# Half-width column groups beside SSD and mLSTM, ScalarE leads for a layer's first operands, and buffer clearing moved behind later weight splits

## The reference, cut to what matters

```python
hn = rms_norm(h, attn_norm_g[l])
proj = hn @ w_in[l]                      # 5056 columns, split among four mixers
y_a = mla_mixer(...)                     # latent attention, 8 heads
y_b = ssd_mixer(...)                     # Mamba-2 SSD, both directions, chunks of 128
y_c = diff_mixer(...)                    # differential attention
y_d = mlstm_mixer(...)                   # mLSTM, both directions, chunks of 128
h = h + concatenate([y_a, y_b, y_c, y_d], -1) @ w_out[l]
hn = rms_norm(h, ffn_norm_g[l])
gate, up = split(hn @ w_ffn_in[l], 2)
h = h + (silu(gate) * up) @ w_ffn_out[l]
```

## Time and profile before

| | us |
|---|---|
| median of three runs | 2256.19 |
| lowest, highest | 2255.35, 2264.37 |
| profiled execution | 2260.73 |
| its span in the trace | 2258.9 |

### The profile page before, as it was taken

One profiled execution on the slowest core, in us unless ns is written; L12 is line 12 of the kernel. 1 busy time (PEld: TensorE's weight loads), 2 busy tenths in 40 slices (PEclk: granted clock), 3 DMA queues, 4 the chain that ended last, 5 costly groups with the idle time before them and its releaser, 6 DMA issues.

```text
span 2258.9 us, 32608 instructions
## 1 busy us (share of the span) xinstructions
PE 2062.5 (91%) x13298; PEld 1781.2 (79%) x13298; DVE 1063.1 (47%) x1653; ACT 820.8 (36%) x1344; POOL 993.5 (44%) x593
## 2 busy tenths in 40 slices
PE   7989998888778999999999999997877789999999
PEld 7978887567657999999989878884555567888887
DVE  8532355565664744442038332555655656444400
ACT  3322343576554222222224322443664633222221
POOL 4455432784311444444434454335861334444444
PEclk9999999999998999999999999999998999999999
DMA  4211111000001222233222111111000012333333
GB/s 161 66 56 57 57 46 67 10 1 19 29 12 37 85 94 87 91 94 94 94 85 84 57 57 57 48 38 56 1 7 31 19 56 94 94 94 98 97 103 112
DMA packets 40035, 143.79 MB, mean 64 GB/s; under 512 B 4432, under 2 KB 4560, under 8 KB 39760
## 3 DMA queue, kind: packets, MB, share of 16 engines
q1 hardware_dynamic: 39888, 141.72, 19.6%
HBM read 139.60 MB, written 2.10 MB: 63 GB/s over the span
## 4 chain that ended last, share of the span: by engine, by line
PE 72%; DVE 11%; ACT 8%; issue 6%; POOL 2%; DMA 1%; SPq 0%; ACTq 0%; DVEq 0%; POOLq 0%
PE pb L850 44%; PE pb L885 6%; PE pb L886 6%; PE pb L887 6%; ACT ebuf L1468 2%; PE pb L1287 1%; DVE rowmax L1926 1%; POOL parts L632 1%; PE pb L1295 1%; ACT rstd L1436 1%; PE pb L1227 1%; DVE proj L1858 1%; PE pb L987 1%; ACT ebuf L1479 1%; ACT parts L1524 1%
## 5 line engine op out<-in xcount | busy, mean ns | idle before, releaser
L632 POOL TENSOR_TENSOR parts<-raw,parts 128x1024 fp32r<-128x1024 f32 x248 | 602.5, 2430 | 829.0 <-ACT parts L1524 828.8
L850 PE MATMUL pb<-mix,parts 128*128 128x264 f32 x4608 | 670.7, 294 | 41.1 <-POOL parts L632 15.7
L850 PEld LDWEIGHTS pb<-mix,parts 128*128 128x128 f32 x4608 | 609.2, 193 | 68.0 <-issue 26.1
L1524 ACT ACTIVATE parts<-raw 128x1024 fp32r<-128x1024 f32 x248 | 262.5, 1058 | 851.1 <-PE pb L850 549.6
L850 PE MATMUL pb<-proj_r,parts 128*128 128x264 f32 x3104 | 429.2, 286 | 0.5 <-POOL parts L632 0.5
L850 PEld LDWEIGHTS pb<-proj_r,parts 128*128 128x128 f32 x3104 | 401.2, 189 | 0.8 <-issue 0.7
L885 PE MATMUL pb<-proj_r,parts 128*128 128x512 f32 x528 | 207.5, 393 | 0.8 <-DVE mbuf L1858 0.8
L887 PE MATMUL pb<-proj_r,parts 128*128 128x512 f32 x528 | 207.7, 393 | 0.0
L886 PE MATMUL pb<-proj_r,parts 128*128 128x512 f32 x496 | 198.1, 399 | 0.0
L1864 DVE TENSOR_TENSOR h<-h,pb 128x528 f32<-128x528 f32 (+1 forms) x48 | 33.2, 693 | 274.9 <-PE pb L850 143.9
L1858 DVE TENSOR_TENSOR mbuf<-pb,rstd 128x528 f32<-128x528 f32 (+1 forms) x44 | 30.8, 700 | 214.8 <-PE pb L850 110.5
(11 more groups left out here) (277 smaller groups left out, 2831.6 us busy)
## 6 DMA issues: line engine op xcount, KB each, us to landing
raw<-w_stream SPq DMA_DIRECT2D x250, 512.0 KB, 3.5
w_head<-w_heads SPq DMA_DIRECT2D x8, 512.0 KB, 4.9
h<-x_t SPq DMA_DIRECT2D x8, 264.0 KB, 6.8
out_t<-h SPq DMA_DIRECT2D x8, 256.0 KB, 4.7
con<-consts SPq DMA_DIRECT2D x1, 1652.5 KB, 10.5
par<-params SPq DMA_DIRECT2D x1, 340.0 KB, 4.3
con<-consts SPq DMA_DIRECT2D x1, 128.0 KB, 7.1
```

Source lines behind the costliest of these rows:

```text
L632: nc.gpsimd.tensor_tensor(parts[:, n % PARTS, 1, :], w, parts[:, n % PARTS, 0, :].bitcast(FP32), ALU.subtract).then_inc(split.sem, 1)
L850: last = nc.tensor.matmul(pb[rows_, 2 * p + a, 0:HALF], lhs_t, rhs[:, a * HALF:(a + 1) * HALF], start=start, stop=stop)
L1524: nc.scalar.activation(parts[:, n % PARTS, 0, :], raw[:, r % RAW, :], ACT.Copy).then_inc(lead_ready.sem, 1)
```

## The change

1. The 25 groups beside SSD and mLSTM are computed half by half. Pieces 0 and 1 of a group now do all eight input tiles for tokens 0 to 263 (one bank), pieces 2 and 3 for tokens 264 to 527 (the other bank). VectorE takes out each half by itself: half 0 at slot 4j+2, half 1 at slot 4j+4. Piece 0 waits for half 0 of the group before, piece 2 for half 1 of it.
2. ScalarE makes the leads of h times gain for both layers (`gain_lead`); VectorE makes only the rests (`gain_rest`). At the end of layer 0 the first four rests stand ahead of the last residual addition.
3. At the start SyncE issues the first weights, then eight columns of the parameters, then all eight tiles of h in a row, then the second weights and the rest. ScalarE loads its table and makes the first weight lead before it waits for parameters.
4. GpSimd clears the six buffers after the rests of slots 2, 4, 5 and 6 of layer 0.

```diff
@@ sync
+            sp.dma_start(raw[:, 0, :], w_stream[0, :, :]).then_inc(loaded[0].sem, 16)
+            sp.dma_start(par[:, 0, 0:KD], params[:, 0, 0:KD]).then_inc(gain_in.sem, 16)
             for k in range(KD):
-                if k < RAW:
-                    sp.dma_start(raw[:, k, :], w_stream[k, :, :]).then_inc(loaded[k].sem, 16)
                 sp.dma_start(h[:, k, :], x_t[:, k, :]).then_inc(x_in[k].sem, 16)
-                if k == 0:
-                    sp.dma_start(par[:, :, :], params).then_inc(par_in.sem, 16)
+            sp.dma_start(raw[:, 1, :], w_stream[1, :, :]).then_inc(loaded[1].sem, 16)
+            sp.dma_start(par[:, 0, KD:N_PARAM], params[:, 0, KD:N_PARAM]).then_inc(par_in.sem, 16)
+            sp.dma_start(par[:, 1:DEPTH, :], params[:, 1:DEPTH, :]).then_inc(par_in.sem, 16)
@@ gpsimd
-            nc.gpsimd.memset(v_tok[:, :], 0.0).then_inc(cleared.sem, 1)
...
-            nc.gpsimd.memset(rows2, 0.0).then_inc(cleared.sem, 1)
+            def clear(s):
+                for buf in ((), (), (mbuf[:, :, :], cols[:, :, :]), (), (v_tok[:, :],), (qh[:, :, :],), (o_tok[:, :, :], rows2))[s]:
+                    nc.gpsimd.memset(buf, 0.0).then_inc(cleared.sem, 1)
...
                     rest(l, s)
+                    if l == 0 and s < 7:
+                        clear(s)
@@ tensor
+            def half_piece(l, g, a, k0):
+                n = l * N_SLOT + g
+                if k0 == 0 and a == 0:
+                    pe.wait_ge(split.sem, n + 1)
+                    if g == G_SSD:
+                        pe.wait_ge(evac.sem, evac.at(l, g))
+                    else:
+                        pe.wait_ge(half_evac.sem, half_evac.at(l, g - G_SSD))
+                elif k0 == 0:
+                    pe.wait_ge(evac.sem, evac.at(l, g))
+                o, cut = pb[:, 2 * bank_pair(g) + a, 0:HALF], slice(a * HALF, (a + 1) * HALF)
+                for k in range(k0, k0 + KD // 2):
+                    w_lead, w_rest = (parts[:, n % PARTS, b, k * P:(k + 1) * P] for b in range(2))
+                    lead, rest = (ap[:, cut] for ap in xg_parts(k))
+                    nc.tensor.matmul(o, w_lead, lead, start=(k == 0), stop=False)
+                    nc.tensor.matmul(o, w_lead, rest, start=False, stop=False)
+                    last = nc.tensor.matmul(o, w_rest, lead, start=False, stop=(k == KD - 1))
+                if k0:
+                    done = w_used if a else half_done
+                    last.then_inc(done.sem, 1)
...
-                    k = (KD // PIECES) * (p % PIECES)
-                    beside(l, G_SSD + p // PIECES, 0, xg_parts, ((k, k + KD // PIECES),))
+                    half_piece(l, G_SSD + p // PIECES, p % PIECES // 2, KD // 2 * (p % 2))
@@ scalar
+            def gain_lead(l, k):
+                if l == 0:
+                    act.wait_ge(x_in[k].sem, 16)
+                else:
+                    act.wait_ge(evac.sem, evac.at(l - 1, G_FOUT + k + 1))
+                nc.scalar.activation(xg_parts(k)[0], h[:, k, :], ACT.Copy, scale=par_at(l, "attn_g", k)).then_inc(xg_lead.sem, 1)
...
-            act.wait_ge(par_in.sem, 16)
+            nc.scalar.preload_act_table_set("natural_log_exp_and_others")
+            lead(0, 0)
+            act.wait_ge(gain_in.sem, 16)
             act.wait_ge(eps_ready.sem, 1)
             for l in range(DEPTH):
                 if l == 0:
-                    nc.scalar.preload_act_table_set("natural_log_exp_and_others")
                     for k in range(KD):
-                        act.wait_ge(x_in[k].sem, 16)
+                        gain_lead(l, k)
+                        if k == 4:
+                            lead(l, 1)
+                    for k in range(KD):
                         residual_square(l, 0, k)
-                        if k < PARTS:
-                            lead(l, k)
-                lead(l, 2)
+                        if k == 3:
+                            lead(l, 2)
+                else:
+                    lead(l, 2)
...
                 for s in range(S_FOUT + 2, N_SLOT + 2):
+                    if s == N_SLOT + 1 and l + 1 < DEPTH:
+                        act.wait_ge(par_in.sem, 32)
+                        act.wait_ge(w_used.sem, w_used.at(l, N_SLOT - 1))
+                        for k in range(KD):
+                            gain_lead(l + 1, k)
                     lead(l, s)
@@ vector
+            def gain_rest(l, k):
+                lead, rest = xg_parts(k)
+                dve.wait_ge(xg_lead.sem, xg_lead.at(l, k + 1))
+                nc.vector.scalar_tensor_tensor(out=rest, in0=h[:, k, :], scalar=par_at(l, "attn_g", k), in1=lead.bitcast(FP32),
+                                               op0=ALU.mult, op1=ALU.subtract).then_inc(xg_ready.sem, 1)
+            def scale_half(l, g, a, dst):
+                cut = slice(a * HALF, (a + 1) * HALF)
+                if a:
+                    dve.wait_ge(w_used.sem, w_used.at(l, g + 1))
+                else:
+                    dve.wait_ge(half_done.sem, half_done.at(l, g - G_SSD + 1))
+                ins = nc.vector.tensor_tensor(dst[:, cut], pb[:, 2 * bank_pair(g) + a, 0:HALF], rstd[:, cut], ALU.mult)
+                released = evac if a else half_evac
+                ins.then_inc(released.sem, 1)
...
-                for k in range(KD):
-                    if l == 0:
-                        dve.wait_ge(x_in[k].sem, 16)
-                    else:
-                        dve.wait_ge(evac.sem, evac.at(l - 1, G_FOUT + k + 1))
-                    gains(l, k, "attn_g", xg_parts)
-                    if l and k == 1:
+                for k in range(KD // 2 if l else 0, KD):
+                    gain_rest(l, k)
+                    if l and k == KD // 2 + 1:
                         add_square(l, 0, KD - 1)
...
                     if p % PIECES == 0 and p:
-                        scale_out(l, g, tile_of(proj, TILE_AT[g]))
+                        scale_half(l, g, 1, tile_of(proj, TILE_AT[g]))
+                    if p % PIECES == 2:
+                        g = G_SSD + p // PIECES
+                        scale_half(l, g, 0, tile_of(proj, TILE_AT[g]))
...
                 for k in range(KD):
+                    if l + 1 < DEPTH and k == KD - 1:
+                        for j in range(KD // 2):
+                            gain_rest(l + 1, j)
                     residual(l, G_FOUT + k, k)
```

More of the change, by code:

```diff
@@ L462, in trunk @@
         eps_ready = signal("eps_ready", 0)
+        gain_in = signal("gain_in", 0)
         par_in = signal("par_in", 0)
@@ L473, in trunk @@
         evac = signal("evac", N_GROUP)
+        half_done = signal("half_done", N_IN - G_SSD)
+        half_evac = signal("half_evac", N_IN - G_SSD)
+        xg_lead = signal("xg_lead", KD)
         xg_ready = signal("xg_ready", 2 * KD)
@@ L2206, in _ @@
                         add_square(l, 0, k)
+                dve.wait_ge(par_in.sem, 32)
                 dve.wait_ge(rs_ready.sem, rs_ready.at(l, RS_A + 1))
@@ L2268, in _ @@
                 out_sums(l, 0, ML_H)
-                scale_out(l, N_IN - 1, tile_of(proj, N_IN - 1))
+                scale_half(l, N_IN - 1, 1, tile_of(proj, N_IN - 1))
                 def value_rest(i):
```

8 lines of the change are left out of this document (1 added, 7 removed).

## The result

The changed kernel takes 2244.5 us in the median of five runs (2238.1 to 2246.2), the kernel before 2256.2 (2251.5 to 2264.4). The ratio is 0.9935, with a 95% interval of 0.9909 to 0.996, so 14.7 us less (9.0 to 20.5). A second comparison with more runs gave 0.9925 (0.9906 to 0.9944), 17.0 us less. The forecast was 2243, 13.8 us less.

What follows compares the result with a forecast made beforehand. TensorE, busy 91% of the span, bounds the kernel, so only its waits and clock count. Halves 7.7, boundary 3.3 and start 2.8 sum to 13.8 us: median 2256.2 becomes 2242.4, said as 2243, own range 2239 to 2247.

Steps and rivals of the forecast that it cites:

- What bounds the kernel: Whole kernel: TensorE, busy 91% of the span; the change wins or loses only by its waits and its clock afterwards.
- The halves: Groups beside SSD and mLSTM: fourteen short waits go (7.8 us), heads give 0.6, added evacuations cost 0.7; together 7.7 us.
- rival b: SSD and mLSTM: removed short waits come back at the next ScalarE and GpSimd chain, leaving half of 7.7; 2247, chance 12%.
- the charge of 0.7 for the added ones: Beside SSD and mLSTM: two evacuations per group delay norm multiplications, between 0 and 3.3 us; 0.7 taken.
- The boundary: Layer 0 to layer 1: ScalarE leads and four rests ahead of the residual addition save 3.0 to 4.5 us; 3.3 taken.
- its 30 matmuls take 6.46 us again: Layer boundary: after 2.8 us idle TensorE loses its clock, so its first 30 matmuls take 6.46 us as before.
- The bound of 4.5: Layer boundary: upper limit of the saving, 4.5 us, if the low clock lasts shorter.
- The start: Program start: sum over features at 25.3 instead of 28.26 us; saving 2.9, 2.8 taken, bounds 0 and 5.
- the landing of the second weights: Program start: second weights, issued behind all of h, land at about 10.9 to 11.5 us; much later and the forecast fails.
- No cost for the clearing and for the order of the matmuls: Memsets fit GpSimd's idle time at the start; the new matmul order beside SSD and mLSTM costs and gains 0.
- Rival a: SSD heads: small copies slip past GpSimd in layer 0 (2238, chance 12%) or meet it in layer 1 (2248, 13%).

Runs made afterwards that it cites:

- the parts alone: Kernel before with one part of the change each: halves 0.9956, order of the matmuls 0.9997, boundary 0.9988, start 0.9996.

## Why the prediction was right, and which terms were off

The total was right, 2243 for 2244.5, and 13.8 us for the 14.7 and 17.0 of the two ratios. The terms were off by +2.3 to +2.7, +1.3 and -1.0 us and some 1.7 us were lost in a place that the forecast didn't name; that the sum still came out so near is in part luck.

**What bounds the kernel.** Right. The stretches got shorter by what TensorE stopped waiting for, by its clock, and at the boundary by a faster supply of operands.

**The halves, 7.7 forecast, 10 measured** (9.9, interval 6 to 14, by the ratio; by the stretches 4.2 + 4.5 for SSD and mLSTM, 0.2 for each head, and about 0.7 for each last wait ahead of `w_head`, by the shortest of these stretches with and without halves where the copies are on VectorE, 57.7 and 58.3). The ratio also holds two things that this sum leaves out: the 1.7 us lost in the rest of layer 1, and the heads with a lost clock, 1.6 us each, which three runs without halves have and none with them. Which waits go was right, and that two stay at the heads (0.64 and 0.65 us). The step that failed is the price: I took a wait for what the view lists, 6.1 us for the twelve up to the sum of squares. Aligning the two timelines instruction by instruction, TensorE gained 5.0 us in layer 0 and 5.3 in layer 1 over these. With two waits of 0.13 us that the view leaves out, that is 0.74 for each, where their idle time is 0.13 to 0.80, 0.46 in the mean. Then 0.9 and 0.7 us were lost again at the wait for the sum of squares, 3.51 us for the 2.61 of the earlier trace rows:

```profile
313.60 2.10 PE L855 MATMUL pb<-sq,con 128*128 128x264 f32 x4 [3.51 <-DVE sq L2216]
```

That is rival b, with 1.6 us of the 3.9 that it was given: a chain through ScalarE and GpSimd that moves by less than TensorE does. A half's evacuation takes 0.43 us, as forecast; the charge of 0.7 for the added ones doesn't show.

**The boundary, 3.3 forecast, 4.6 measured.** The idle time was right (2.8 forecast, 2.60 measured), and so was its cause, the residual addition behind four rests of which the first waits for GpSimd. The Trainium skill's rule (SBUF — State Buffer, section "SBUF: two separate sides") of a port pair locked between the two engines decided this step; the rows above agree (2.39 us for the first rest, 0.76 for the next), and so does the fifth rest in the run with the addition moved up (2.86 us). The step that failed is "its 30 matmuls take 6.46 us again": they took 5.2 (the 31st starts at 1154.17), which is nearly the whole difference. The windows of the kernel before (us, busy us of PE, PEld, DVE, ACT, POOL, then the granted clock) show that these 30 were slow for two reasons:

```profile
1166.60:1169.00 2.40, 2.31 (x10) 2.31 (x11) 2.33 (x6) 0.00 (x0) 0.00 (x0) 0.50 0.60 213
1169.00:1171.00 2.00, 1.98 (x10) 1.67 (x9) 1.97 (x4) 0.00 (x0) 0.00 (x0) 0.50 0.00 0
1171.00:1173.00 2.00, 1.96 (x14) 1.69 (x13) 1.93 (x4) 0.00 (x0) 0.00 (x0) 0.95 0.00 0
1173.00:1175.00 2.00, 1.59 (x11) 1.22 (x10) 1.93 (x5) 0.00 (x0) 0.00 (x0) 1.00 0.00 0
```

Up to about 1171 the clock is at its lower level. From then on it is at 2.4 GHz, and still only 14 and 11 matmuls start in 2 us: VectorE, busy all the time, hands over a tile every 1.2 us. I took the merged row for a stretch of slow clock alone. In the changed kernel (us, busy PE, granted clock, DMA) the low level lasts some 3.2 us, and then nothing holds the matmuls up:

```profile
1149.00:1151.00 2.00, 2.00 (x9) 0.50 0.00 0
1151.00:1153.00 2.00, 2.00 (x14) 0.70 0.00 0
1153.00:1155.00 2.00, 2.00 (x18) 1.00 0.32 66
```

The bound of 4.5 named for "if the low clock lasts shorter" was near the right value, but a part of its reason was missing: without leads on VectorE the rests come faster.

**The start, 2.8 forecast, 1.8 in the mean** (2.4 in this profile). The path was as forecast: first matmul at 8.36 us (8.5), sum at 25.89 (25.3), the first of the sums of squares that meets GpSimd among them. The step that was mis-sized is the landing of the second weights: 12.0 instead of 10.9 to 11.5, and in two of the six profiles 12.8 and 13.7. The prediction named this as what would make it fail, but gave it no width; and it left out that the longer wait could cost TensorE its clock, which in these two took another 1.0 us.

**No cost for the clearing and for the order of the matmuls.** Both right, each by its own run.

**Rival a** is real in kind. Between the first two profiles it came the lucky way: layer 0's head went from 10.8 to 5.2 us, and the profiled run took 2238.1, the rival's 2238. But the median didn't move with it. The changed kernel has the short copies in both layers in every profile, and the kernel before has one long head in each of its two profiles, 5.4 us each. If that is usual for it, removing it is a part of the gain that the parts alone would show too, since none of them has slow copies; the ratios of the order and the boundary alone (0.9997 and 0.9988) leave no room for 5.4 us, or for the 3.8 that remain beside a lost clock of 1.6. That is why I count it as unexplained, not as an effect. It widens the gap between the two profiled spans: 5.6 of their 22.6 us are this head.

The parts by their stretches, 10.4 + 4.6 + 1.8 = 16.8 us, less the 1.7 in the rest of layer 1, make 15.1; by the ratios of their runs they make 9.9 + 2.7 + 0.9 = 13.5. The ratios of the whole give 14.7 and 17.0. All of these lie inside the intervals of both (9.0 to 20.5 and 12.7 to 21.2).

## What to carry to other kernels

Price a removed wait by the distance between the starts around it, with and without, and not by the listed idle time; then look for the next chain that doesn't move with the engine, and take its wait off. Read a merged row of slow matmuls beside the granted clock of short windows before calling it slow clock: it can be a supplier's pace. An operand stock ahead of a meeting between VectorE and GpSimd is worth its delay: with the addition moved up and the stock gone the wait came back, and it shrank to 0.83 us only when the first rests were moved ahead of GpSimd's subtraction and the last sums behind all rests. A wait shorter than 1 us can cost the clock too; read the granted clock behind each before calling it cheap.

## What the runs showed of the hardware

- The length of a wait alone doesn't tell what TensorE's clock does. Waits of 0.83 and 0.84 us at the boundary left it at 2.4 GHz (36 matmuls in 4.65 us), and so did 2.22 us at the start (66 in 8.34 us). Waits of 0.84 to 0.94 us at layer 1's SSD head took it to 1.2 in three runs (24 matmuls in 4.72 us in one, not 3.2), and so did 2.36 us at the start (66 in 9.77). 2.60 us at the boundary took it to 1.2 for some 3.2 us (9 matmuls in the first 2).
- Eight copies of 64 x 12 and 64 x 6 elements take 1.0 us on ScalarE. On VectorE beside GpSimd's tensor operations they take 4.3 us when two pass per GpSimd operation and 7.7 when one does, in the same program.
- A two-input VectorE operation of 0.7 us that begins within a GpSimd subtraction of 2.4 us ends some 0.5 us after it (the first rest at the boundary, 2.39 us).
- The second 512 KB of weights, issued behind h at 5.5 to 6.1 us, were ready at 11.4 to 13.7 us in six profiles of the same order of transfers.
- A stretch of attention and FFN that no edit touched took 772.5 to 781.3 us, with a granted clock of 0.93 to 0.97 in its first half where it was 773.3 and 0.90 to 0.94 where it was 781.3.
